# Requesting the experts' down weights on another engine's DMA queue in a hybrid block

## The chip, the cores and the metric

The kernel runs on one core of a Trainium2 chip. The metric is the device time of one execution in microseconds (us). The kernel before took 1451.0 us, the median of three runs (1449.7 to 1451.66).

A core has five engines that run their own instruction streams and meet at semaphores: PE (TensorE, matmuls; its weight loads are shown as PEld), DVE (VectorE), ACT (ScalarE), POOL (GpSimd) and SP (SyncE, which here only issues transfers). A transfer (DMA) is issued by SP, ACT or POOL and carried out by the core's 16 DMA engines.

## The reference, cut to what matters

One block on 1024 tokens of width 1024: a mixer (a gated delta rule beside a causal convolution), a mixture of experts, a gate, and a norm. The change lies in the mixture of experts:

```python
group_p = softmax(xf @ w_group_router); g_w, g_idx = top_k(group_p, 1)
in_group = (xf @ w_expert_router) of the chosen group of 8 experts
e_w, e_idx = top_k(softmax(in_group), 2)          # 2 of 64 experts for each token
gate = g_w * e_w / sum(e_w)
...
def expert_block(args):                            # x_blk: tokens of one expert
    x_blk, e = args
    a, b = jnp.split(x_blk @ w_up[e], 2, axis=-1)  # 1024 -> 2 x 256
    return (jax.nn.silu(a) * b) @ w_down[e]        # 256 -> 1024
...
y = segment_sum(yb * buf_w[:, None], buf_tok, num_segments=N)
```

All is float32. Per expert w_up is 1024 x 512 (2 MB) and w_down 256 x 1024 (1 MB), so the 64 experts bring 192 MB from HBM, once each.

## The kernel before

The program has stages one behind the other: norm and input projection, the delta rule, output projection and router logits, the routing tables, then the expert stage (`c7`, from line 1832), then the gate and final norm (`c8`, from line 2203).

In the expert stage the 64 experts are taken as 32 pairs; pair p holds the experts p and p + 32. Each expert has 64 token slots, so that one half of the 128 columns belongs to each. Work of one pair on PE, in this order: U(p), 16 up matmuls (line 2121) of 128x512 (the profile counts each as two); T(p+1), 8 transposes of the next pair's tokens (line 2110); 2 transposes of the hidden values (line 2130); D(p), 8 down matmuls (line 2142). ACT does, in order: `silu` of half of U(p) (line 1978), its half of the copy of T(p+1) (line 1974), and `result`, its half of the copy of D(p) out of PSUM (line 1984). DVE has the other halves. POOL gathers the tokens (line 1919) and scatters the results to `y_rows` (line 1925), by indirect transfers.

All weight buffers are double: `wup[k]` (in the `wup` ring) and `wdn[k]` (in `zT` for k = 0, in `convT` for k = 1) with k = p mod 2, each with two halves c = 0, 1, one for each expert of the pair. The pairs 0 and 1 are requested during the routing stage (lines 1622 to 1626). From then on SP waits for the end of U(p) and requests the two up halves of pair p+2 (`fetch_up`), waits for the end of D(p) and requests the two down halves of pair p+2 (`fetch_down`), and so on for p = 0 to 29 (`fetch_pairs`, line 1874). U(p) waits for `s_up[k]`, D(p) for `s_dn[k]`.

An expert with more than 64 tokens has overflow blocks. They are worked off between pair 15 and pair 16 (`MID` = 8 loop turns of two pairs); in this run there is one. Its weights `wup_x` and `wdn_x` are loaded at the start of the stage.

Behind its last pair SP requests the ten weight rows of the gate stage (line 1900, 512 KB each). The first two can go at once; the others wait for buffers. ACT splits them into high parts (`weights_high`, line 1995) in a fixed order with its last pairs: silu(30), tokens(31), weights 0 and 1, result(30), weights 2 to 4, silu(31), result(31), weights 5 to 9 (lines 2015 to 2026).

Of the kernel before, what the change touches and what calls it, by code (L numbers as in the profile page):

```python
# [14 lines left out]
ds = bass.ds  # L15
# [30 lines left out]
def hybrid_block_kernel(nc, x, p, g_mix, w_in, w_conv_qkv, a_log, dt_bias, g_gdn_out, b_glu,  # L46
# [20 lines left out]
    NPR = NE // 2  # L67
# [11 lines left out]
    def sem(name):  # L79
        return top.enter_context(nc.semaphore(name))  # L80
# [3 lines left out]
    def wait_alone(eng, sem_, value):  # L84

        eng.wait_ge(sem_, value)
        eng.sem_inc(s_turn, 1)
# [7 lines left out]
    with top:  # L95
# [48 lines left out]
        with ExitStack() as c1:  # L144
# [13 lines left out]
            @blk.sync  # L158
            def _(sp):
                for t in range(NT):  # L160
                    sp.dma_start(xs[:, t, :], x[0, t * P:(t + 1) * P, :]).then_inc(s_x[t], 16)
                    if t == 1:
                        sp.dma_start(gmix[:], g_mix[0].rearrange("(p j) -> p j", j=NJ)).then_inc(s_loaded, 16)
                        sp.dma_start(wraw[0][:], w_in_p[:, :, GOFF:GOFF + P]).then_inc(s_w[0], 16)
                sp.dma_start(wraw[1][:], w_in_p[:, :, GOFF + CF:GOFF + CF + P]).then_inc(s_w[1], 16)
# [525 lines left out]
        G2 = range(2)  # L691
# [876 lines left out]
        NS = 2  # L1568
        NJF = FE // P
        s_up = [sem(f"s_up{k}") for k in range(NS)]  # L1570
        s_dn = [sem(f"s_dn{k}") for k in range(NS)]
        wring = ExitStack()
        wup = [[sb(f"wup{k}{c}", [P, NJ, 2 * FE], ctx=wring) for c in G2] for k in range(NS)]
        wdn = [[t[:, c * NJF:(c + 1) * NJF, :] for c in G2] for t in (zT, convT)]
        up_p = w_up[0].rearrange("e (p j) n -> p e j n", j=NJ)
        dn_p = w_down[0].rearrange("e (p j) n -> p e j n", j=NJF)

        def fetch_up(sp, k, c, e):
            sp.dma_start(wup[k][c][:], up_p[:, e, :, :]).then_inc(s_up[k], 16)

        def fetch_down(sp, k, c, e):
            sp.dma_start(wdn[k][c], dn_p[:, e, :, :]).then_inc(s_dn[k], 16)
        s_iota, s_rv, s_ra, s_rp = sem("s_iota"), sem("s_rv"), sem("s_ra"), sem("s_rp")
        W8 = [P, NT, NG]
        with ExitStack() as c6:
# [215 lines left out]
        def wrow(j):  # L1801

            j -= p.shape[3] // P
            return w_ple_gate[0, j * P:(j + 1) * P, :] if j >= 0 else w_ple_proj[0, p.shape[3] + j * P:p.shape[3] + (j + 1) * P, :]
# [6 lines left out]
        s_T, s_x0, s_x1, s_u, s_sil, s_h, s_hT, s_hx, s_d, s_y0, s_y1 = (  # L1811
            sem("moe_" + n) for n in ("T", "x0", "x1", "u", "sil", "h", "hT", "hx", "d", "y0", "y1"))
# [16 lines left out]
        def fetch_rows(sp, t, g):  # L1829
            for y, k, there in ((yy[g], 0, s_fy[g]), (yz[g], 1, s_fz[g])):  # L1830
                sp.dma_start(y.unsqueeze(1), y_tok[ds(t * P, P), k:k + 1, :]).then_inc(there, 16)
        with ExitStack() as c7:
# [33 lines left out]
            @blk.sync  # L1866
            def _(sp):
                def fetch_over(v):
                    e = sp.value_load(eov[0:1, ds(v, 1)], min_val=0, max_val=NE - 1)
                    wait_alone(sp, s_od, v + 1)  # L1870
                    sp.dma_start(wup_x[:], up_p[:, ds(e, 1), :, :]).then_inc(s_oup, 16)
                    sp.dma_start(wdn_x[:], dn_p[:, ds(e, 1), :, :]).then_inc(s_odn, 16)

                def fetch_pairs(first_, last_):
                    with sp.Fori(first_, last_) as i:
                        for k in range(NS):
                            p = NS * i + k
                            wait_alone(sp, s_u, p + 1)
                            for c in G2:
                                fetch_up(sp, k, c, ds(p + NS + NPR * c, 1))  # L1880
                            wait_alone(sp, s_d, p + 1)
                            for c in G2:
                                fetch_down(sp, k, c, ds(p + NS + NPR * c, 1))

                n_over = sp.value_load(nov[0:1, 0:1], min_val=0, max_val=NOV)
                sp.sem_inc(s_od, 1)
                with sp.If(n_over > 0):
                    fetch_over(0)
                fetch_pairs(0, MID)
                with sp.If(n_over > 1):  # L1890
                    with sp.Fori(1, n_over) as v:
                        fetch_over(v)
                fetch_pairs(MID, NIT - 1)

                for j in range(NWJ):
                    if j >= NRAW:
                        sp.wait_ge(s_wg_lo, j - NRAW + 1)
                    elif j >= NAHEAD:
                        sp.wait_ge(s_T, NPR - NRAW + j + 1)
                    sp.dma_start(wg_raw[j % NRAW], wrow(j)).then_inc(s_wg[j % NRAW], 16)  # L1900
                    if j == NAHEAD:
                        for g in G2:
                            sp.dma_start(pin[g][:], p_tok[0, 0, g * P:(g + 1) * P, :]).then_inc(s_fp[g], 16)
                    if j == NRAW:
                        sp.wait_ge(s_d, NPR - 1)
                        sp.dma_start(gP, g_ple.partition_broadcast(P)).then_inc(s_gfin, 16)
                        sp.dma_start(gF, g_final.unsqueeze(0).partition_broadcast(P)).then_inc(s_gfin, 16)
                for k in range(NS):
                    sp.wait_ge(s_sto[k], 16 * NIT)
                sp.wait_ge(s_d, NPR)  # L1910
                for g in G2:
                    fetch_rows(sp, g, g)
# [57 lines left out]
            @blk.scalar  # L1970
            def _(act):
                def tokens(k, p):
                    act.wait_ge(s_T, p + 1)
                    nc.scalar.activation(xgT[k][:, 0:HJ, :], ps_x[0][:], ACT.Copy).then_inc(s_x0, 1)

                def silu(k, p, rows=slice(0, P)):
                    act.wait_ge(s_u, p + 1)
                    nc.scalar.activation(sil[k][rows], ps_u[k][rows, 0:FE], ACT.Silu).then_inc(s_sil, 1)  # L1978

                def result(k, p, free, rows=slice(0, P)):  # L1980
                    act.wait_ge(s_d, p + 1)
                    if free is not None:
                        act.wait_ge(s_sto[k], free)
                    nc.scalar.activation(ye[k][rows, HF[0]], ps_y[rows, 0, :], ACT.Copy).then_inc(s_y0, 1)

                def pair(i, k, last=False):
                    p = NS * i + k
                    silu(k, p)
                    if not last:
                        tokens(1 - k, p + 1)  # L1990
                    result(k, p, None if isinstance(i, int) and i == 0 else 16 * i)

                def weights_high(j):
                    act.wait_ge(s_wg[j % NRAW], 16 * (j // NRAW + 1))
                    nc.scalar.activation(wg[0][j], wg_raw[j % NRAW], ACT.Copy).then_inc(s_wg_hi, 1)

                tokens(0, 0)
                for k in range(NS):
                    pair(0, k)
                with act.Fori(1, MID) as i:  # L2000
                    for k in range(NS):
                        pair(i, k)
                n_over = act.value_load(nov[0:1, 0:1], min_val=0, max_val=NOV)
                with act.If(n_over > 0):
                    with act.Fori(0, n_over) as v:
                        act.wait_ge(s_oT, v + 1)
                        nc.scalar.activation(xgT_x[:, 0:HJ, :], ps_x[0][:, :, 0:C], ACT.Copy).then_inc(s_ox0, 1)
                        act.wait_ge(s_ou, v + 1)
                        nc.scalar.activation(sil_x[:], ps_u[0][HC[0], 0:FE], ACT.Silu).then_inc(s_osil, 1)
                        act.wait_ge(s_od, v + 2)  # L2010
                        nc.scalar.activation(ye_x[:, HF[0]], ps_y[HC[0], 0, :], ACT.Copy).then_inc(s_oy0, 1)
                with act.Fori(MID, NIT - 1) as i:
                    for k in range(NS):
                        pair(i, k)
                i, p = NIT - 1, NPR - NS
                silu(0, p)
                tokens(1, p + 1)
                for j in range(0, 2):
                    weights_high(j)
                result(0, p, 16 * i)  # L2020
                for j in range(2, N_X + 2):
                    weights_high(j)
                silu(1, p + 1)
                result(1, p + 1, 16 * i)
                for j in range(N_X + 2, NWJ):
                    weights_high(j)
# [397 lines left out]
```

## Time and profile before

| | us |
|---|---|
| median of three runs | 1451.0 |
| span of the profiled execution, first to last instruction | 1440.7 |
| expert stage, first U to last D | 752.0 to 1281.8 of the span |
| PE busy in the whole span | 1168.7 (81%) |
| weights of the up product, transfers | 64 of 2048 KB, and 1 for the overflow |
| weights of the down product, transfers | 64 of 1024 KB, and 1 for the overflow |
| moved in all by DMA | 272.67 MB |

The page does not give the profiled execution's own time beside its span; what lies around the span is 1451.0 - 1440.7 = 10.3 us if that execution took the median time. Read the page's slices first: each is 36 us long, and those of the expert stage (21 to 35) show whether PE or the DMA engines are full. Then the windows say the same in GB/s, the waits say for whom PE stood still, and the timeline gives the order of events inside one pair. A line "SPq ... DMA_DIRECT2D x2" is the issue of two transfers, not their duration: the transfer goes on long after it.

### The profile page before, as it was taken

To read this page: it belongs to the slowest core of one execution; us is meant where nothing else is said; L and a number is where in the kernel's file an instruction comes from. 1 tells how busy PE (TensorE), PEld (TensorE's weight loads), DVE (VectorE), ACT (ScalarE), POOL (GpSimd) and SP (SyncE) were. 2 spreads that over 40 slices of the span, in tenths; PEclk is the share of its full clock that TensorE was granted. 3 is DMA by queue.
4 is the path that set the end of the run, shared out by engine and by line. 5 is a ranking of instruction groups with operands and counts; after the bars stand their busy time and mean duration, and the time that the engine had idled before them with its cause. 6 is when DMAs were issued, how large, how long until landed. Compare 5 with 4: busy or idle time off the path is not lost. (4 is left out here: it accounts for less than half of the span.)

```text
span 1440.7 us, 17450 instructions
## 1 busy us (share of the span) xinstructions
PE 1168.7 (81%) x6323; PEld 774.1 (54%) x6324; DVE 635.6 (44%) x899; ACT 324.8 (23%) x691; POOL 242.4 (17%) x340
## 2 busy tenths in 40 slices
PE   4999999998578776999229888778888878748997
PEld 3888888895377665788213333223233333316775
DVE  7398989983476564522651111111111111144553
ACT  5221221214445443321101100101011100033222
POOL 2100000003445642000011111111112111111111
PEclk7999999976689899999559999989999999978999
DMA  4212111100000010411658999999799999962321
GB/s 148 60 44 58 44 44 44 44 0 0 1 1 2 4 57 17 154 70 61 267 207 336 427 428 425 421 406 413 305 419 428 426 425 417 417 227 75 108 95 44
DMA packets 68059, 272.67 MB, mean 189 GB/s; under 512 B 11625, under 2 KB 38442, under 8 KB 51370
## 3 DMA queue, kind: packets, MB, share of 16 engines
q1 hardware_dynamic: 56096, 254.30, 44.3%
q0 software_dynamic: 9456, 16.80, 3.1%
q10 hardware_dynamic: 2458, 0.92, 0.3%
q8 instruction: 30, 0.49, 0.1%
q14 instruction: 19, 0.16, 0.0%
HBM read 264.12 MB, written 25.43 MB: 201 GB/s over the span
## 5 line engine op out<-in xcount | busy, mean ns | idle before, releaser
L2121 PE MATMUL ps_u<-wup,xgT 128*64 128x512 f32 x1024 | 256.2, 658 | 60.6 <-DMA wup<-in_w_up_dram 58.0
L2121 PEld LDWEIGHTS ps_u<-wup,xgT 128*64 128x64 f32 x1024 | 85.7, 150 | 230.0 <-issue 228.8
L92 PE MATMUL ps_b<-n_hi,wh 128*128 128x512 f32 x384 | 150.5, 392 | 6.1 <-DVEq L405 6.1
L92 PE MATMUL ps_b<-n_lo,wh 128*128 128x512 f32 x384 | 150.2, 391 | 0.0
L92 PE MATMUL ps_b<-n_hi,wl 128*128 128x512 f32 x384 | 150.1, 391 | 0.0
L2041 DVE TENSOR_TENSOR hb<-sil,ps_u 128x256 f32<-128x256 f32 x32 | 13.5, 421 | 298.6 <-ACT sil L1978 298.6
L92 PEld LDWEIGHTS ps_b<-n_hi,wh 128*128 128x128 f32 x384 | 72.6, 189 | 21.4 <-ACTq L40 6.5
L92 PEld LDWEIGHTS ps_b<-n_hi,wl 128*128 128x128 f32 x384 | 72.6, 189 | 15.3
L92 PEld LDWEIGHTS ps_b<-n_lo,wh 128*128 128x128 f32 x384 | 72.7, 189 | 15.1
L1978 ACT ACTIVATE sil<-ps_u 128x256 f32<-128x256 f32 x32 | 12.2, 383 | 286.3 <-PE ps_u L2121 286.3
L423 DVE SCALAR_TENSOR_TENSOR convT<-upad,vecT,convT 128x1024 f32 (+1 forms) x60 | 76.7, 1278 | 0.0
L2053 DVE COPY qkvT<-ps_y 128x512 f32<-128x512 f32 x32 | 22.1, 690 | 122.1 <-PE ps_y L2142 122.1
L2142 PE MATMUL ps_y<-convT,hT 128*64 128x512 f32 x256 | 62.8, 635 | 12.2 <-DVE hT L2047 12.2
L423 DVE SCALAR_TENSOR_TENSOR odd<-upad,vecT,odd 128x1024 f32<-128x1024 f32 x56 | 71.5, 1277 | 0.0
L1923 POOL COPY si<-sidx 128x1 int32 (+1 forms) x32 | 6.6, 207 | 379.9 <-DVE qkvT L2053 379.9
L2142 PE MATMUL ps_y<-zT,hT 128*64 128x512 f32 x256 | 58.5, 598 | 11.0 <-DVE hT L2047 11.0
L357 ACT ACTIVATE wh<-wraw 128x1024 fp32r<-128x1024 f32 x24 | 25.5, 1062 | 172.4 <-PE ps_b L92 172.4
L92 PE MATMUL ps_o<-wo_hi,mix_hi 128*128 128x512 f32 x128 | 52.3, 408 | 6.6 <-DVE wo_lo L1485 6.4
L2110 PEld LDWEIGHTS ps_xg<-ident,xg 128*128 128x128 f32 x256 | 31.6, 195 | 46.2 <-issue 24.3
L601 POOL TENSOR_TENSOR GT<-sm_g,tri 128x512 f32<-128x512 f32 x8 | 8.0, 1038 | 287.3 <-DVE sm_g L657 287.3
L2110 PE MATMUL ps_xg<-ident,xg 128*128 128x128 f32 x256 | 37.9, 292 | 20.8 <-DMA xg<-xn_rows,gi 20.8
L92 PE MATMUL ps_gate<-wg_hi,hx_hi 128*128 128x512 f32 x128 | 51.7, 404 | 2.4 <-DVE hx_lo L2319 2.4
(368 smaller groups left out, 2034.6 us busy)
## 6 DMA issues: line engine op xcount, KB each, us to landing
wup<-in_w_up_dram SPq DMA_DIRECT2D x64, 2048.0 KB, 17.7
zT<-in_w_down_dram SPq DMA_DIRECT2D x32, 1024.0 KB, 17.3
convT<-in_w_down_dram SPq DMA_DIRECT2D x32, 1024.0 KB
wraw<-in_w_in_dram SPq DMA_DIRECT2D x25, 512.0 KB, 4.0
convT<-y_rows SPq DMA_DIRECT2D x16, 512.0 KB, 5.2
qkvT<-in_x_dram SPq DMA_DIRECT2D x8, 512.0 KB, 7.2
qkvT<-in_w_out_dram SPq DMA_DIRECT2D x8, 512.0 KB, 4.9
xr<-in_x_dram SPq DMA_DIRECT2D x8, 512.0 KB, 3.2
```

Of the source, the lines that this page charges most:

```text
L92: ins = nc.tensor.matmul(ps, lhs[a], rhs[b], start=first and k == 0, stop=last and k == 2)
L357: nc.scalar.activation(wh[n % 2][:], wraw[n % 2][:], ACT.Copy).then_inc(*a_proj(f"hi{n}"))
L423: ins = nc.vector.scalar_tensor_tensor(dst, src, DW(k, i), dst, ALU.mult, ALU.add)
L601: nc.gpsimd.tensor_tensor(GT[:, of_tile(t), :], sm["g"][:, t, :].unsqueeze(2).to_broadcast(F4), tri[:].unsqueeze(1).to_broadcast(F4), ALU. ...
L1923: nc.gpsimd.tensor_copy(si[k][:], sidx[:, p]).then_inc(s_idx, 1)
L1978: nc.scalar.activation(sil[k][rows], ps_u[k][rows, 0:FE], ACT.Silu).then_inc(s_sil, 1)
L2041: nc.vector.tensor_tensor(hb[k][rows], sil[k][rows], ps_u[k][rows, FE:2 * FE], ALU.mult).then_inc(s_h, 1)
L2053: nc.vector.tensor_copy(ye[k][rows, HF[1]], ps_y[rows, 1, :]).then_inc(s_y1, 1)
L2110: last = nc.tensor.transpose(ps_x[j // HJ][:, j % HJ, :], xg[k][:, j:D:NJ], ident[:])
L2121: last = nc.tensor.matmul(ps_u[k][HC[c], :], xgT[k][:, j, HC[c]], wup[k][c][:, j, :], start=j == 0, stop=j == NJ - 1)
L2142: last = nc.tensor.matmul(ps_y[HC[c], h, :], hT[k][:, f, HC[c]], wdn[k][c][:, f, HF[h]], start=f == 0, stop=f == NJF - 1)
```

## The change

`fetch_down` is called by ACT instead of SP. ACT calls it right behind `result(k, p)` in `pair`, for the same pairs (p = 0 to 29). SP no longer waits for the end of D(p). The transfers, their sizes, sources, targets and semaphores are the same.

```diff
-        def fetch_down(sp, k, c, e):
-            sp.dma_start(wdn[k][c], dn_p[:, e, :, :]).then_inc(s_dn[k], 16)
+        def fetch_down(eng, k, c, e):
+            eng.dma_start(wdn[k][c], dn_p[:, e, :, :]).then_inc(s_dn[k], 16)
...
                             wait_alone(sp, s_u, p + 1)
                             for c in G2:
                                 fetch_up(sp, k, c, ds(p + NS + NPR * c, 1))
-                            wait_alone(sp, s_d, p + 1)
-                            for c in G2:
-                                fetch_down(sp, k, c, ds(p + NS + NPR * c, 1))
...
                     result(k, p, None if isinstance(i, int) and i == 0 else 16 * i)
+                    for c in G2:
+                        fetch_down(act, k, c, ds(p + NS + NPR * c, 1))
```

On SP, in the body of the loop over pairs (two pairs a turn), before:

```order
L1579 DMA wup<-in_w_up_dram 128x4096
L1582 ISA
L1582 DMA zT<-in_w_down_dram 128x2048
L1582 ISA
L1582 DMA zT<-in_w_down_dram 128x2048
L1579 ISA
L1579 DMA wup<-in_w_up_dram 128x4096
L1579 ISA
L1579 DMA wup<-in_w_up_dram 128x4096
L1582 ISA
L1582 DMA convT<-in_w_down_dram 128x2048
```

The same place on SP after:

```order
L1579 DMA wup<-in_w_up_dram 128x4096
L1579 ISA
L1579 DMA wup<-in_w_up_dram 128x4096
L1579 ISA
L1579 DMA wup<-in_w_up_dram 128x4096
L1579 ISA
L1579 DMA wup<-in_w_up_dram 128x4096
L1875 REGISTER_ALU
L1875 COMPARE_AND_BRANCH
```

SP's queue now holds up weights alone, one pair's behind the other's. On ACT, in the body of its loop over pairs, before (`sil` is the silu, `xgT` the copy of the tokens, `qkvT<-ps_y` the result):

```order
L1978 ACTIVATE sil<-ps_u 128x256
L1973 REGISTER_ALU
L1974 ACTIVATE xgT<-ps_xg 128x512
L1983 REGISTER_ALU
L1984 ACTIVATE qkvT<-ps_y 128x512
L1978 ACTIVATE sil<-ps_u 128x256
```

and after:

```order
L1975 ACTIVATE sil<-ps_u 128x256
L1970 REGISTER_ALU
L1971 ACTIVATE xgT<-ps_xg 128x512
L1980 REGISTER_ALU
L1981 ACTIVATE qkvT<-ps_y 128x512
L1582 ISA
L1582 DMA zT<-in_w_down_dram 128x2048
L1582 ISA
L1582 DMA zT<-in_w_down_dram 128x2048
L1975 ACTIVATE sil<-ps_u 128x256
```

Two issues stand between the result of one pair and the silu of the next. The instructions of PE, DVE and POOL stand as before.

## Rows read from the trace of the kernel before

**Rows 1.** The page's 40 slices of 36 us: busy tenths, PE clock, DMA share and rate.

```profile
PE   4999999998578776999229888778888878748997
PEclk7999999976689899999559999989999999978999
DMA  4212111100000010411658999999799999962321
GB/s 148 60 44 58 44 44 44 44 0 0 1 1 2 4 57 17 154 70 61 267 207 336 427 428 425 421 406 413 305 419 428 426 425 417 417 227 75 108 95 44
```

**Rows 2.** Windows of the expert stage: length, busy by engine, clock, DMA share, GB/s.

```profile
762.00:810.00 48.00, 41.00 (x200) 16.28 (x198) 8.53 (x16) 6.07 (x12) 8.72 (x15) 0.99 0.99 408
810.00:1005.00 195.00, 157.87 (x684) 60.17 (x686) 24.91 (x47) 18.33 (x35) 27.86 (x45) 0.92 1.01 420
1022.00:1031.30 9.30, 7.72 (x36) 2.62 (x36) 0.68 (x1) 0.81 (x2) 1.34 (x3) 1.00 0.20 81
1032.00:1094.00 62.00, 55.16 (x252) 20.45 (x250) 10.25 (x20) 7.50 (x14) 11.05 (x19) 0.94 1.00 413
1094.00:1261.00 167.00, 135.09 (x580) 51.86 (x580) 20.65 (x39) 15.18 (x29) 23.19 (x38) 0.92 1.01 422
```

**Rows 3.** Waits of PE, 762 to 1270 us: total, times, longest.

```profile
PE ps_u L2121 <- DMA wup<-in_w_up_dram: 58.0, 22, 4.2
PE ps_y L2142 <- DVE hT L2047: 22.6, 31, 0.9
```

**Rows 4.** Timeline of pairs 14 and 15, start and duration, [idle before <- releaser].

```profile
978.42 8.78 PE L2121 MATMUL ps_u<-wup,xgT 128*64 128x512 f32 x32 [2.90 <-DMA wup<-in_w_up_dram]
...
987.46 0.86 SPq L1579 DMA_DIRECT2D wup<-in_w_up_dram  x2
...
989.41 3.65 PE L2142 MATMUL ps_y<-zT,hT 128*64 128x512 f32 x16 [0.68 <-DVE hT L2047]
993.20 0.60 ACT L1984 ACTIVATE qkvT<-ps_y 128x512 f32<-128x512 f32 x1 [4.26 <-PE ps_y L2142]
...
993.31 0.85 SPq L1582 DMA_DIRECT2D zT<-in_w_down_dram  x2
...
994.99 1.51 PE L2121 MATMUL ps_u<-wup,xgT 128*64 128x512 f32 x6 [1.92 <-DMA wup<-in_w_up_dram]
```

**Rows 5.** DMA, 1100 to 1240 us: share by queue, then KB each and landing.

```profile
q1 hardware_dynamic: 4948, 54.09, 91.5%
q0 software_dynamic: 2547, 5.06, 9.3%
...
wup<-in_w_up_dram SPq DMA_DIRECT2D x18, 2048.0 KB, 19.8
...
zT<-in_w_down_dram SPq DMA_DIRECT2D x8, 1024.0 KB, 21.3
...
xg<-xn_rows,gi POOLq DMA_INDIRECT x8, 14.0
```

**Rows 6.** Timeline of a pair at full speed, pair 2 into pair 3.

```profile
780.36 0.60 ACT L1984 ACTIVATE qkvT<-ps_y 128x512 f32<-128x512 f32 x1 [4.18 <-PE ps_y L2142]
...
787.23 0.38 ACT L1978 ACTIVATE sil<-ps_u 128x256 f32<-128x256 f32 x1 [6.27 <-PE ps_u L2121]
```

**Rows 7.** Timeline around the overflow block and behind it.

```profile
1023.95 7.09 PE L2121 MATMUL ps_u<-wup,xgT 128*64 128x512 f32 x32 [1.58 <-DVE qkvT L2083]
...
1031.28 0.86 SPq L1579 DMA_DIRECT2D wup<-in_w_up_dram  x2
...
1033.16 1.05 POOL L1919 DMA_INDIRECT xg<-xn_rows,gi  x1 [0.91 <-POOL gi L1917]
...
1046.07 1.16 PE L2110 MATMUL ps_xg<-ident,xg 128*128 128x128 f32 x8 [2.31 <-DMA xg<-xn_rows,gi]
...
1062.09 0.87 SPq L1579 DMA_DIRECT2D wup<-in_w_up_dram  x2
```

**Rows 8.** Timeline of the end of the stage.

```profile
1261.28 7.09 PE L2121 MATMUL ps_u<-wup,xgT 128*64 128x512 f32 x32 [1.35 <-DMA wup<-in_w_up_dram]
1267.19 1.06 ACT L1995 ACTIVATE wg_hi<-qkvT 128x1024 fp32r<-128x1024 f32 x1 [11.40 <-DMA qkvT<-in_w_ple_proj_dram]
...
1272.91 1.06 ACT L1995 ACTIVATE wg_hi<-qkvT 128x1024 fp32r<-128x1024 f32 x1 [0.19 <-DMA qkvT<-in_w_ple_gate_dram]
...
1273.87 0.36 ACT L1978 ACTIVATE sil<-ps_u 128x256 f32<-128x256 f32 x1
...
1276.82 5.01 PE L2142 MATMUL ps_y<-convT,hT 128*64 128x512 f32 x16 [0.52 <-DVE hT L2047]
```

## Prediction

> **What bounds the kernel now.** I read the page's slices first. From slice 22 to slice 34 the DMA row stands at 9 with one dent, and the rate at 406 to 428 GB/s, while PE has room [rows 1]. The windows say it closer: 420 GB/s at a share of 1.01 from 810 to 1005 us, and 422 GB/s at 1.01 from 1094 to 1261 us [rows 2]. The dent is the overflow block: 81 GB/s from 1022 to 1031.3 us. So the expert stage is two stretches in which the DMA engines are full, with some 9 us between them in which they are nearly idle because everything requested has landed and the next request comes only at the end of U(16), at 1031.28 us [rows 7].
>
> Next the waits of PE: 58.0 us in 22 waits for up weights, and none for down weights; before D it waits only for DVE's copy [rows 3]. Then the order of one pair [rows 4]: U(14) starts when its up weights land (978.42), the up request of pair 16 goes out at 987.46, D(14) runs from 989.41, its down request goes out at 993.31, U(15) starts on landing at 994.99, some 16.6 us behind U(14).
>
> Last, the order of transfers. All weights stand in one queue, SP's, in the order up(p), down(p), up(p+1), down(p+1). U(p) can start when up(p) is down; down(p) moves behind it, while U(p) runs. Both halves of a down transfer are 2 x 1024 KB = 2.10 MB, at 422 GB/s 5.0 us. U and the transposes take 10 to 11 us from the start of U to the start of D (978.42 to 989.41 [rows 4]), so down(p) lands before D(p) wants it. This order is the best one for a stage bound by transfers: what is wanted first moves first.
>
> **The change, part by part.**
>
> *Issue time.* SP loses a wait and two issues for each pair; it was not waited for. ACT gains two issues behind each result. On SP two such issues took 0.85 us [rows 4]; taken as the same on ACT, or even double, they fit between the result at 780.36 + 0.60 us and the silu at 787.23 us, for which ACT stood idle 6.27 us in a pair at full speed [rows 6]. Cost: 0. Were the cover gone, each pair would pay 0.85 us only in a stretch where PE sets the pace. The request itself goes out up to 1 us later than now, since it stands behind the copy; down weights have 5 us and more to spare.
>
> *Order of the transfers, the term that counts.* Down(p) is requested at the end of D(p-2), that is one period (16.6 us) and PE's wait before U(p) starts. Now it stands behind up(p) in the queue and cannot move. On a queue of its own it can. What happens to two queues with work is shown by POOL's gathers: they are issued when some 20 us of weights are queued, and land in 14.0 us, while a down transfer that is issued on SP's queue lands in 21.3 us [rows 5]. So the queues share the engines, and the later queue does not wait for the earlier one. And the rate stays at 422 GB/s with both in use [rows 2, 5], so sharing costs no bandwidth.
>
> Then down(p), 5.0 us of work, is served between parts of up(p-1) and up(p). Even at one part in three it needs about 3 x 5.0 = 15 us of the 16.6 + 1.9 us (PE's wait in rows 4) it has before U(p) starts. So all of it moves ahead of the last bytes of up(p), and U(p) starts 5.0 us later than it does now. In the middle of a full stretch that costs nothing further: each pair is later by the same 5.0 us, the period stays what the bytes make it. The price is paid once at the end of a stretch, where the bytes that used to move under the last U now move ahead of it.
>
> First stretch: U(15), D(15) and the overflow block come 5.0 us later, and so does the request at the end of U(16) that starts the engines again. They had nothing to do in the meantime: the dent grows from 9.3 to about 14 us. Cost: +5.0 us. Bounds: 0, if down(15) still lands last; +6.3 us, if part of down(16), requested 1.7 us before U(15) starts, moves ahead too, and the request reaches an engine without delay (1.7 us at half the engines is 0.9 us; I allow 1.3).
>
> The Trainium skill, "DMA: Bandwidth & Descriptors", section "Queues, rings and completion order", says that each DMA engine goes round between the queues it has work for, and drains a whole packet of one before it switches. The gathers' 14.0 us against 21.3 us agree with it. By it the sum would be the same 5.0 us, since an up half and a down half would alternate, and both down halves pass before the second up half.
>
> Second stretch: U(31) comes another 5.0 us later. But here the end is not set by U(31). ACT stands before weights 0, which land at 1267.19 us behind down(31), goes through weights 1 to 4 until 1272.91 + 1.06 us, and does silu(31) at 1273.87 us only then; U(31) had ended at 1261.28 + 7.09 = 1268.4 us [rows 8]. The landing of these rows is the end of all bytes, which a change of order does not move. Now: U(31) starts at 1261.28 + 5.0 + 5.0 = 1271.3, ends 1278.4; weights 4 are done at 1273.97 + 5.0 = 1279.0. So silu(31) follows at 1279.0, 0 us beyond the first stretch's shift. If the wait before U(31) is longer, the granted clock may be lower (it is 0.92 on the mean of the full stretches [rows 2]): U then takes 8.78 us, as U(14) did behind a wait of 2.90 us [rows 4], and silu(31) comes at 1280.1, +1.1 us. I take +0.3, bounds 0 and +1.1.
>
> *Gathers.* A third queue in use delays gathers by at most one down half at a time, 2.5 us. In a full stretch they have room. Behind the overflow block they have none: the gather issued at 1033.16 us makes PE wait 2.31 us, until 1046.07 [rows 7]. The engines then have, from 1032 us [rows 2], two pairs' weights, 12.6 MB or 30 us at 422 GB/s, and 33 us with the gathers and scatters between them (weights are 54.09 of 59.15 MB [rows 5]), until 1065 us. The next up request comes at 1062.09 us [rows 7], just in time, so a delay of PE there can go through in part. Down(18) is requested at about 1037 us and stands in SP's queue behind up(18) now; after, it may go before the gather. Bounds 0 and +2.5 us; I take +0.5, nearer to 0, since down halves are queued there today too and some 2 us are to spare.
>
> Sum: 5.0 + 0.3 + 0.5 + 0 = +5.8 us. The profiled span would go from 1440.7 to 1446.5 us. With the 10.3 us around it, the median goes from 1451.0 to 1456.8 us, +0.4%. Its own range, from the bounds of the four terms where the mechanism holds, is +4.5 to +10 us: 1455.5 to 1461.
>
> **The rivals.**
>
> *No change.* The order does not matter: the bytes are the same, the engines are full, and down(15) lands in time either way. For it speaks that the rate can't rise and that PE's waits are for bytes; against it the 9.3 us of nearly idle engines behind the first stretch, which turn any later end of U(15) into time. It needs a sharing in which down(p) gets next to nothing of the engines beside up transfers: to pass whole it needs 5.0 of 18.5 us, 27%, and any less costs in proportion. Time 1451. The Trainium skill, the same page, section "Issuing engines are not separate DMA queues", says that requests from several engines run on the same 16 DMA engines and save only the sequencer's time. Taken by itself that gives no change; it says nothing of what lands first.
>
> *Faster.* SP's queue is served first whenever it has work, so up(p) no longer stands behind down(p-1) either. Place: up(15) would land up to 5.0 us earlier, and U(15) with it; D(15) still has 5 us to spare for its own weights. The dent shrinks from 9.3 to 4.3 us, time 1451.0 - 5.0 = 1446. Against it: the gathers on a second queue are not served last (14.0 us against 21.3 us [rows 5]).
>
> *Slower by more: the engines run dry.* At the start of U(p) there are queued, instead of the rest of down(p), up(p+1) and down(p+1), only the last two: about 15 us. The next request comes at the end of U(p), 8.8 us later. That leaves some 5 us, where now it is 10. If the 16 engines are further apart than that, or gathers come late for each pair, each of the 22 pairs that wait today loses about 0.7 us: 15 us on top, 1472. For it: landings differ from pair to pair (waits up to 4.2 us [rows 3]); against it: 5 us is more than that.
>
> **How the numbers follow.** A difference under 0.2% (2.9 us) can't be told from none here. The forecast has 0.62, no change 0.18, faster 0.08, dry engines 0.12. The forecast's range lies above 0.2% almost wholly (I leave 0.03 of it below): slower 0.59 + 0.12 = 0.71, same 0.21 with it, faster 0.08. The range that holds 8 in 10 takes the forecast's, most of no change, and part of dry engines: 1450.5 to 1464.
>
> **What would show it.** In the changed trace: down transfers on ACT's queue that land in 10 to 16 us instead of 21.3; up landings about as before (19.8), since request and start of U shift together; the period of a full stretch within 0.3 us of now; rates of 420 and 422 GB/s; U(16) at about 1029 us instead of 1023.95; the idle dent 14 us long; U(31) at about 1271 us, with silu(31) at 1279. I am wrong on the mechanism if U(16) starts within 1.5 us of 1024, wrong on its one-time price if the period has grown, and wrong on the end if silu(31) waits for U(31) by several us.

## The result, and the profile after

| | kernel before | changed kernel |
|---|---|---|
| median of 20 runs each | 1449.68 us | 1455.14 us |
| ratio, 95% interval | | 1.0044 [1.0027, 1.0061] |
| span of the profiled execution | 1440.7 us | 1446.0 us |

The change costs 0.44%, 6.4 us of 1449.7. The forecast was +5.8 us. The place of the price holds, at the overflow block; what it is made of does not, so the nearness of the two numbers is in part luck, as the profile after and the experiments show. One of the 20 executions of the kernel before took 3338.41 us and is left out of the ratio.

In every execution of the runs the time lies 1.7 to 2.1 us above its span (1447.81 and 1446.0 us for the profiled one of the changed kernel), not 10.3 us. So the profiled execution of the kernel before took about 1442.5 us (an estimate), and both profiled executions are some 7 us faster than the median of their kernel. Each profile below is one execution.

The DMA rate of the full stretches is what it was, with a longer dent in the middle (the page's slices, to read against [rows 1]):

```profile
DMA  4212111100000011421648999999699999972321
GB/s 148 59 44 58 44 44 44 44 0 1 1 1 2 8 53 23 147 73 58 283 190 355 426 427 423 418 408 403 257 425 411 428 426 413 417 252 75 116 95 44
```

The waits of PE, 762 to 1275 us, against [rows 3]:

```profile
PE ps_xg L2109 <- DMA xg<-xn_rows,gi: 43.6, 22, 3.2
PE ps_u L2120 <- DMA wup<-in_w_up_dram: 25.6, 14, 2.9
```

This the prediction had not seen: PE now waits for tokens in 22 pairs, and less for up weights. The transfers of 1100 to 1240 us, against [rows 5], say why:

```profile
q1 hardware_dynamic: 2490, 36.31, 61.8%
q10 hardware_dynamic: 2436, 17.71, 30.3%
q0 software_dynamic: 2441, 4.57, 8.5%
...
wup<-in_w_up_dram SPq DMA_DIRECT2D x16, 2048.0 KB, 18.3
zT<-in_w_down_dram ACTq DMA_DIRECT2D x10, 1024.0 KB, 16.5
convT<-in_w_down_dram ACTq DMA_DIRECT2D x8, 1024.0 KB, 18.2
y_rows<-qkvT,si POOLq DMA_INDIRECT x9, 16.4
xg<-xn_rows,gi POOLq DMA_INDIRECT x9, 22.9
```

Down weights land in 16.5 to 18.2 us instead of 21.3. Gathers, which now share with two queues, land in 22.9 us instead of 14.0.

The overflow block, from pair 15 to pair 16 (timeline, against [rows 4, 7]):

```profile
999.00 7.09 PE L2120 MATMUL ps_u<-wup,xgT 128*64 128x512 f32 x32 [1.47 <-DMA wup<-in_w_up_dram]
...
1008.09 1.16 PE L2109 MATMUL ps_xg<-ident,xg 128*128 128x128 f32 x8 [1.99 <-DMA xg<-xn_rows,gi]
...
1014.20 0.85 ACTq L1582 DMA_DIRECT2D convT<-in_w_down_dram  x2
...
1016.21 0.38 ACT L2006 ACTIVATE xgT_x<-ps_xg 128x256 f32<-128x256 f32 x1 [1.56 <-issue]
1016.65 7.08 PE L2164 MATMUL ps_u<-wup_x,xgT_x 128*64 128x512 f32 x16 [1.61 <-ACT xgT_x L2006]
...
1030.77 7.09 PE L2120 MATMUL ps_u<-wup,xgT 128*64 128x512 f32 x32 [1.58 <-DVE qkvT L2082]
```

The last rows of the dent, in windows of 1 us (the last two numbers are the DMA share and GB/s). Kernel before:

```profile
1028.00:1029.00 1.00, 1.00 (x8) 0.31 (x5) 0.00 (x0) 0.00 (x0) 0.00 (x0) 1.00 0.12 49
...
1030.00:1031.00 1.00, 1.00 (x7) 0.18 (x3) 0.00 (x0) 0.00 (x0) 0.15 (x1) 1.00 0.12 49
1031.00:1032.00 1.00, 1.00 (x10) 0.94 (x8) 0.42 (x1) 0.38 (x1) 0.93 (x1) 1.00 0.06 25
1032.00:1033.00 1.00, 0.56 (x4) 0.32 (x2) 0.84 (x3) 0.60 (x1) 0.24 (x2) 1.00 1.26 229
```

Changed kernel:

```profile
1033.00:1034.00 1.00, 1.00 (x8) 0.41 (x6) 0.00 (x0) 0.00 (x0) 0.00 (x0) 1.00 0.10 41
1034.00:1035.00 1.00, 1.00 (x6) 0.30 (x4) 0.00 (x0) 0.00 (x0) 0.00 (x0) 1.00 0.02 8
...
1035.00:1038.00 3.00, 3.00 (x16) 0.96 (x12) 0.00 (x0) 0.10 (x1) 1.35 (x3) 1.00 0.01 0
1038.00:1039.00 1.00, 1.00 (x9) 0.88 (x9) 0.44 (x2) 0.30 (x2) 0.57 (x1) 1.00 0.01 0
1039.00:1040.00 1.00, 0.38 (x2) 0.19 (x2) 1.00 (x2) 0.58 (x1) 0.48 (x1) 1.00 1.23 246
...
1024.00:1039.00 15.00, 12.30 (x51) 4.70 (x52) 1.83 (x5) 1.14 (x4) 2.85 (x5) 1.00 0.14 58
```

A share of 0.12 of 16 engines is the work of two engines; the view gives the mean alone, so that it is the same two all along is inferred. In the kernel before such a rest is at work until about half a microsecond before the next request is served (0.12 up to 1031 us, 0.06 in the next window). In the changed kernel all 16 stand all but still from 1034 to 1039 us, 5 us (shares of 0.03 or less). The time in which most engines have nothing to do is 10 us long in the kernel before (1022 to 1032 us, mean share 0.19) and 15 us in the changed kernel (1024 to 1039 us). That is where the price lies.

The stage starts at another time in each execution (U(0) at 752.0 us before, 753.4 in the changed kernel), so the table below counts from the start of U(0), read from the timelines.

| us from U(0), profiled execution | U(15) | overflow U | U(16) | U(31) |
|---|---|---|---|---|
| kernel before | 243.0 | 257.9 | 272.0 | 509.3 |
| changed | 245.6 | 263.2 | 277.4 | 518.2 |
| early gathers on the changed kernel | 244.8 | 262.0 | 277.7 | 517.5 |
| early gathers on the kernel before | 242.4 | 257.3 | 271.4 | 509.0 |
| down on ACT, first half | 246.2 | 263.2 | 277.4 | 514.9 |
| down on ACT, second half | 242.6 | 257.5 | 271.6 | 513.2 |
| up transfers split, changed | 249.2 | 267.8 | 283.6 | 526.0 |
| all on ACT's queue | 244.2 | 261.4 | 277.3 | 519.5 |
| all on ACT's queue, gate weights too | 243.8 | 261.1 | 276.9 | 516.4 |
| pair 15 down first | 248.3 | 264.5 | 278.6 | 514.9 |
| pair 31 down first | 242.7 | 257.6 | 271.7 | 514.3 |

The experiments behind these rows follow. One pattern runs through them: each kernel of this table whose U(16) comes 4.9 to 11.7 us later costs 5.4 to 10.1 us, and none whose U(16) is in time costs anything clear of the scatter. The next table says what makes U(16) late, by the rows of each timeline: idle time before a matmul group, and the group's own duration. "Slower U" is a U that took 8.4 to 10.0 us where it took 7.1 in the kernel before.

| us later than in the kernel before | up to U(15) | U(15) to overflow U | overflow U to U(16) | sum |
|---|---|---|---|---|
| changed | 2.6 | 2.8: tokens 2.0, ACT 0.7 | 0.0 | 5.4 |
| down on ACT, first half | 3.2 | 2.2: tokens 1.4, ACT 0.7 | 0.0 | 5.4 |
| early gathers on the changed kernel | 1.8 | 2.3: slower U 1.6, ACT 0.7 | 1.6: slower U | 5.7 |
| up transfers split, changed | 6.2 | 3.7: slower U 3.0, ACT 0.7 | 1.8: slower U | 11.7 |
| all on ACT's queue, gate weights too | 0.8 | 2.4: slower U 1.7, ACT 0.7 | 1.7: slower U | 4.9 |
| pair 15 down first | 5.3 | 1.3: slower U | 0.0 | 6.6 |

The end of the stage, against [rows 8]:

```profile
1271.62 10.09 PE L2120 MATMUL ps_u<-wup,xgT 128*64 128x512 f32 x32 [2.88 <-DMA wup<-in_w_up_dram]
1274.02 1.06 ACT L1994 ACTIVATE wg_hi<-qkvT 128x1024 fp32r<-128x1024 f32 x1 [9.42 <-DMA qkvT<-in_w_ple_proj_dram]
...
1281.74 0.38 ACT L1975 ACTIVATE sil<-ps_u 128x256 f32<-128x256 f32 x1 [0.64 <-PE ps_u L2120]
...
1283.77 3.65 PE L2141 MATMUL ps_y<-convT,hT 128*64 128x512 f32 x16 [0.52 <-DVE hT L2046]
```

### The profile page after: what moved, and what is told of

It is laid out like the page before. It is cut to its first block and busy times, and to the rows that moved or that the text cites. A ratio compares the mean times of both kernels' runs of the same rounds, so it can differ in the third digit from the quotient of the medians.

```text
span 1446.0 us, 17414 instructions
## 1 busy us (share of the span) xinstructions
PE 1165.4 (81%) x6323; PEld 769.8 (53%) x6324; DVE 636.7 (44%) x899; ACT 325.1 (22%) x691; POOL 241.5 (17%) x340
## 5 line engine op out<-in xcount | busy, mean ns | idle before, releaser
L2120 PE MATMUL ps_u<-wup,xgT 128*64 128x512 f32 x1024 | 239.2, 622 | 28.0 <-DMA wup<-in_w_up_dram 25.6
L2120 PEld LDWEIGHTS ps_u<-wup,xgT 128*64 128x64 f32 x1024 | 77.7, 144 | 186.6 <-issue 185.4
L2109 PE MATMUL ps_xg<-ident,xg 128*128 128x128 f32 x256 | 40.9, 308 | 62.3 <-DMA xg<-xn_rows,gi 62.3
L2141 PE MATMUL ps_y<-zT,hT 128*64 128x512 f32 x256 | 76.3, 751 | 12.4 <-DVE hT L2046 12.4
## 6 DMA issues: line engine op xcount, KB each, us to landing
wup<-in_w_up_dram SPq DMA_DIRECT2D x64, 2048.0 KB, 16.8
zT<-in_w_down_dram ACTq DMA_DIRECT2D x30, 1024.0 KB, 16.5
```

The lines of the kernel that those rows point to most:

```text
L2109: last = nc.tensor.transpose(ps_x[j // HJ][:, j % HJ, :], xg[k][:, j:D:NJ], ident[:])
L2120: last = nc.tensor.matmul(ps_u[k][HC[c], :], xgT[k][:, j, HC[c]], wup[k][c][:, j, :], start=j == 0, stop=j == NJ - 1)
L2141: last = nc.tensor.matmul(ps_y[HC[c], h, :], hT[k][:, f, HC[c]], wdn[k][c][:, f, HF[h]], start=f == 0, stop=f == NJF - 1)
```

## The experiments

The expectations below name four theories. O: the price is that of the order of the transfers, down(p) moving ahead of up(p). G: it is that of the late gathers. P: each pair pays a part. I: issuing transfers on ACT costs by itself.

**In which stretch is it paid?** The loop turns ahead of the overflow block request down weights in one way, those behind it in the other:

```diff
-                def fetch_pairs(first_, last_):
+                def fetch_pairs(first_, last_, downs):
...
-                fetch_pairs(0, MID)
+                fetch_pairs(0, MID, False)
...
-                fetch_pairs(MID, NIT - 1)
+                fetch_pairs(MID, NIT - 1, True)
```

(with `fetch_down` called in ACT's `pair` for the turns where SP does not; the second kernel has the two the other way round).

> Down weights are requested on ACT's queue for pairs 2 to 17 only (the loop turns ahead of the overflow block), on SP's for 18 to 31. Theories O and G: the whole price is paid at the overflow block, where the DMA engines run empty, so +5 to +7 us as with the full change, and U(16) at about 1030 us. Rival P (a price for each pair): half of the full change, +2 to +3 us.

> Down weights are requested on ACT's queue for pairs 18 to 31 only, on SP's for 2 to 17. Theory O: U(31) starts 5 us later but ACT stands before the gate weights anyway, so 0 to +1.5 us, U(16) at 1024 us as before. Rival P (a price for each pair): +2 to +3 us.

Measured: first half 1.0057 [1.0026, 1.0088], second half 1.0000 [0.9975, 1.0026]. The price is paid in the first half, at the overflow block; in the second there is none to within some 4 us. A price of 2 to 3 us in each half falls, since the first half alone costs at least 3.8 us, and nothing shows that ACT's issues cost in the loop. In the second half U(31) came 3.9 us later (509.3 to 513.2) and PE waited 30.1 us for tokens, without an effect on the time that could be told from none.

**Are the late gathers the cause?** POOL's `turn` gathers pair p, then scatters pair p-3 instead of p-2:

```diff
-                    fetch_tokens(k, ds(p, 1), 2 * p - NS + 1)
-                    wait_alone(pool, s_y0, p - NS + 1)
-                    wait_alone(pool, s_y1, p - NS + 1)
-                    scatter(k, ds(p - NS, 1), 2 * p - NS + 2)
+                    gather(k, p)
+                    scattered(1 - k, p - NS - 1, 2 * p - NS + 1)
```

> The changed kernel with one thing more: POOL requests the tokens of pair p ahead of the scatter of pair p-3 and its wait for D(p-3), instead of behind them, so gathers go out 6 to 9 us earlier. Theory O (order of the weights): what costs is that down(p) moves ahead of up(p), +5 us once at the overflow block. Gathers in time only turn PE's waits for tokens (43.6 us in the changed kernel) back into waits for up weights; U(16) still starts at 1028 to 1029 us and the time stays 4 to 6 us above the kernel before. Theory G (late gathers): what costs is that tokens come late, so D(p) and the next down request come late; with tokens in time the kernel goes back to within 1 us of the kernel before.

> The kernel before with the earlier gathers alone. Both theories: PE's one wait for tokens behind the overflow block (2.31 us) is the only one that can go, and up weights set the pace elsewhere: 0 to 2 us faster than the kernel before. A change beyond 3 us would mean that gathers set something that the waits of before do not show.

Measured: on the changed kernel 1.0046 [1.0020, 1.0072], on the kernel before 0.9994 [0.9976, 1.0011]. The waits of PE in the changed kernel with early gathers, 750 to 1300 us, have none for tokens:

```profile
PE ps_u L2136 <- DMA wup<-in_w_up_dram: 64.6, 26, 3.8
PE ps_y L2157 <- DVE hT L2062: 23.0, 32, 0.8
```

So 43.6 us of waits for tokens can be taken away and the time stays: the forecast of theory G, within 1 us of the kernel before, fails. But the experiment changed more than PE's waits for tokens. In its profile gathers still take longer than in the kernel before (18.1 us for 14.0), down weights land almost as late as there, and the scatters take 20.9 us:

```profile
convT<-in_w_down_dram ACTq DMA_DIRECT2D x8, 1024.0 KB, 19.8
y_rows<-qkvT,si POOLq DMA_INDIRECT x9, 20.9
xg<-xn_rows,gi POOLq DMA_INDIRECT x8, 18.1
```

U(15) is only 1.8 us late, the 2.0 us for tokens are gone, and in their place stand two slower U's at the block (3.2 us). So the order of the weights does not carry the 5.7 us of this kernel by itself either, and what share of the changed kernel's price the gathers have is not settled by it.

**Order alone, on one queue.** SP requests pair 15, that one pair, in the other order (called with p = 13; the up halves then go out behind the end of D(13) too, about 6 us later than in the kernel before, while the engines stay full: a share of 1.01 from 980 to 1000 us):

```diff
+                def down_first(p):
+                    k = p % NS
+                    sp.wait_ge(s_u, p + 1)
+                    sp.wait_ge(s_d, p + 1)
+                    for c in G2:
+                        fetch_down(sp, k, c, p + NS + NPR * c)
+                    for c in G2:
+                        fetch_up(sp, k, c, p + NS + NPR * c)
```

> The kernel before, all requests on SP's queue, with one difference: for pair 15, the last ahead of the overflow block, SP waits for the end of U(13) and of D(13) and requests the down halves ahead of the up halves. Nothing is issued on ACT, gathers share with one queue. Theory O: this alone makes U(15) land 5.0 us later and brings the whole price of the first stretch: U(16) 4 to 6 us later against the stage's start, all 16 DMA engines idle for some 4 us before the next request, time +3 to +6 us. Theory G and rival I (gathers, or issuing on ACT): no change, 0 to +1 us.

> The same swap for pair 31, the last of the stage, alone. Theory O: U(31) starts 4 to 6 us later but ACT's silu(31) stands behind gate weights 2 to 4 anyway: 0 to +2 us. A rival in which any late U counts in full: +5 us.

Measured: pair 15 1.0037 [1.0018, 1.0057], pair 31 0.9979 [0.9956, 1.0001]. U(15) with pair 15 swapped:

```profile
1000.89 8.41 PE L2142 MATMUL ps_u<-wup,xgT 128*64 128x512 f32 x32 [9.66 <-DMA wup<-in_w_up_dram]
```

It starts 5.3 us later against U(0) (248.3 and 243.0), the 5.0 us of the sum, and U(16) 6.6 us later, the rest being a slower U(15) (8.41 for 7.09 us). As theory O expected, all engines stand all but still before the next request, from 1033 to 1038 us (a share of 0.02). One pair's order, with no second queue and nothing on ACT, costs 0.37% (0.18 to 0.57), about what the whole change does. At pair 31 the same shift (514.3 and 509.3, 5.0 us) costs nothing, since ACT reaches silu(31) late in any case. This shows that the order alone can bring such a price, and that a late U counts at the block and not at the end of the stage. It does not show that the order brings the whole of it in the changed kernel, where U(15) is 2.6 us late and not 5.3.

**The share that down weights get.** Each up transfer in two, of 8 KB pieces instead of 16 KB:

```diff
-            sp.dma_start(wup[k][c][:], up_p[:, e, :, :]).then_inc(s_up[k], 16)
+            for j in (0, NJ // 2):
+                sp.dma_start(wup[k][c][:, j:j + NJ // 2, :], up_p[:, e, j:j + NJ // 2, :]).then_inc(s_up[k], 16)
```

> The changed kernel with each up transfer of 2048 KB issued as two of 1024 KB (four of eight rows of a partition each, so the pieces are 8 KB long instead of 16 KB). Theory O+: queues take turns piece by piece, so down weights get an even share instead of a third and pass even earlier; the order price stays at +5 us, while gathers wait for shorter pieces and come back from 22.9 towards 14 to 17 us. Theory G: with gathers back in time the price goes, 0 to +2 us. If turns go by whole transfers the same holds; if they go by time or bytes, gathers stay at 23 us.

Measured: 1.0070 [1.0044, 1.0097]. Landings, 1100 to 1240 us:

```profile
convT<-in_w_down_dram ACTq DMA_DIRECT2D x8, 1024.0 KB, 12.2
y_rows<-qkvT,si POOLq DMA_INDIRECT x8, 10.3
xg<-xn_rows,gi POOLq DMA_INDIRECT x8, 13.2
```

Gathers are back at 13.2 us and down weights land in 12.2 instead of 18.2: with pieces of 8 KB on both queues down weights get the larger share. U(15) starts 6.2 us late (249.2) instead of 2.6. Gathers in time and yet a price: again against the forecast of G, for O. Whether the price is higher than the changed kernel's is not clear of the intervals, and of the 11.7 us by which U(16) is late 4.7 us are slower U's. The landings fit queues that take turns by piece; whole transfers as turns were not told apart from it by this run. Nor do the pieces alone set them: with early gathers the pieces are 16 and 8 KB as in the changed kernel, and gathers landed in 18.1 us there, not in 22.9.

**One queue again, on ACT.** ACT requests up weights too, behind its copy of the tokens; in the second kernel also the gate weights 0 to 2 and the first tiles of p:

```diff
+                    for c in G2:
+                        fetch_up(act, k, c, ds(p + NS + NPR * c, 1))
                     result(k, p, None if isinstance(i, int) and i == 0 else 16 * i)
                     for c in G2:
                         fetch_down(act, k, c, ds(p + NS + NPR * c, 1))
```

> All weights of the loop on one queue again, but ACT's: ACT requests the up halves of pair p+2 behind its copy of the tokens, the down halves behind its result; SP only keeps the waits. Theories O and G (two queues are the cause): order and gathers as before, down landings about 21 us, gathers about 14 us, U(16) within 1.5 us of 1024, time 0 to +2 us (ACT is held for its issues at the overflow block, 0.7 us in the changed kernel). Rival I (issuing on ACT is the cause): as slow as the changed kernel or slower, +5 us and more, since ACT now issues three times the bytes and twice the transfers.

> All weights of the loop on ACT's queue, and the gate weights 0 to 2 and the first two tiles of p behind them on the same queue, so that nothing passes up(31) from another queue at the end. Theory O: what was left of the price in the run without this (U(31) waited 5.2 us, silu(31) 10.7 us late) goes; what remains is ACT's 0.7 us at the overflow block and the clock that PE happens to have there: 0 to +4 us, between the kernel before and the run without this. Rival I (issuing on ACT itself costs): stays at +8 us.

Measured: 1.0058 [1.0034, 1.0082] and 1.0044 [1.0021, 1.0067]. I had expected 0 to +2 and 0 to +4 us: missed. Landings are as in the kernel before (down 20.3 to 21.1 us, gathers 14.2 and 13.8), U(15) is 1.2 and 0.8 us late, and yet U(16) is 5.3 and 4.9 us late. The timeline of the second kernel:

```profile
995.61 8.78 PE L2126 MATMUL ps_u<-wup,xgT 128*64 128x512 f32 x32 [2.09 <-DMA wup<-in_w_up_dram]
...
1012.44 0.38 ACT L2007 ACTIVATE xgT_x<-ps_xg 128x256 f32<-128x256 f32 x1 [1.54 <-issue]
1012.88 8.78 PE L2170 MATMUL ps_u<-wup_x,xgT_x 128*64 128x512 f32 x16 [1.60 <-ACT xgT_x L2007]
```

Three things are added: 0.8 us at U(15), 0.7 us because ACT issues its two down requests before it copies the overflow block's tokens (idle before U of the block 1.60 us, before 0.90), and 1.7 us twice, since both U(15) and the block's U took 8.78 us where they took 7.09 and 7.05 in the kernel before. 0.8 + 0.7 + 1.7 + 1.7 = 4.9 us. Behind U(16) there is one more: its up request goes out 8.4 us behind its start, not 7.3 as in the kernel before (1031.28 - 1023.95), since ACT issues it behind its copy. So issuing on ACT costs in this place (0.7 and 1.0 us shown), and the clock that PE has there 3.4 us. The granted clock (the third number from the end) during U(15) in the kernel before:

```profile
994.99:1002.10 7.11, 7.11 (x33) 2.71 (x34) 0.00 (x0) 0.00 (x0) 2.26 (x3) 1.00 0.99 407
```

and in the second kernel of this pair during U(15) and the block's U:

```profile
995.61:1004.40 8.79, 8.79 (x33) 3.19 (x33) 0.00 (x0) 0.00 (x0) 2.26 (x3) 0.81 0.99 409
1012.88:1021.66 8.78, 8.77 (x16) 2.48 (x16) 0.00 (x0) 0.00 (x0) 0.67 (x2) 0.81 1.00 397
```

1.00 is the upper of its two levels (2.4 GHz) throughout, 0.81 is a mean, with a part of the time at the lower one (1.2 GHz, shown as 0.50). Why PE is at the lower level there in both of these kernels and with early gathers (0.81 as well), and not in the kernel before, is open: its waits before U alternate between about 2 and 4 us in the kernel before and are 2 to 3 us in the two kernels here, and each kernel has one profile.

Rival I had forecast the size of both results (+5 us and more, +8 us; measured 8.4 and 6.4 us), so these two runs do not speak against it. What does is the second half (ACT issues there, 1.0000) and pair 15 (nothing on ACT, 1.0037): issuing on ACT is not the whole cause.

**The overflow block elsewhere.** `MID = 2`, so that it comes between pairs 3 and 4:

```diff
-            MID = NIT // 2
+            MID = 2
```

> The kernel before with the overflow block worked off between pairs 3 and 4 (MID = 2) instead of between 15 and 16. There the engines are not yet waited for (PE's first wait for up weights is at 810 us). The engines' idle dent of 9.3 us should be shorter, since up(4), down(4), up(5), down(5) are mostly still queued when the block begins: by all theories 3 to 9 us faster than the kernel before.

> The changed kernel with the overflow block between pairs 3 and 4. Theory O: the stretch ahead of the block is not bound by transfers, so nothing is paid there; at the end ACT's wait for gate weights covers the shift. The difference to the kernel before with the same move falls from +6.4 us to 0 to +2 us. Rival P (a price for each pair) and theory G in the form that late gathers cost each pair: the difference stays at +5 to +7 us.

Measured: 1.0025 [1.0004, 1.0046] and 1.0069 [1.0040, 1.0097]. Both misses, and of one kind. I took the dent of 9.3 us as idle time to be had. But the last two engines have almost none of it; that this is why nothing was gained is argued, and no run isolates it. With the block moved, such late work is still going on when the next request goes out at 836.13 us:

```profile
835.00:836.00 1.00, 1.00 (x7) 0.19 (x3) 0.00 (x0) 0.07 (x1) 0.18 (x1) 1.00 0.16 66
836.00:837.00 1.00, 1.00 (x9) 0.88 (x8) 0.42 (x1) 0.31 (x1) 0.45 (x1) 1.00 0.08 33
```

while in the changed kernel all engines stand all but still there too, for some 5 us:

```profile
825.00:830.00 5.00, 5.00 (x26) 1.61 (x22) 0.00 (x0) 0.00 (x0) 2.16 (x4) 1.00 0.02 2
```

The changed kernel's PE waits as early as U(3) (1.57 us for up weights) and T(4) (2.08 us for tokens), so the stretch ahead of the block is bound by transfers there, against my expectation, and its price is paid: U(4), the first behind the block, is 6.0 us late (75.8 us from U(0) for 69.8), and the two kernels' runs are 4.8 us apart on the mean (1454.5 and 1449.7 us), about what it is at the old place.

**A version that beats both.** The end of the stage in [rows 8] shows U(31) done at 1268.4 us and ACT elsewhere. On ACT, silu(31) goes ahead of gate weights 2 to 4, on DVE `hidden` and `hidden_turned` likewise:

```diff
+                silu(1, p + 1)
                 for j in range(2, N_X + 2):
                     weights_high(j)
-                silu(1, p + 1)
```

> The kernel before with silu(31) on ACT, and hidden(31) with its turned copy on DVE, ahead of the gate weights 2 to 4 instead of behind them. U(31) ends at 1268.4 us in the kernel before and silu(31) starts at 1273.87 us only because ACT is at those weights. Expected by every theory: D(31) ends 4 to 5.5 us earlier, the gate weights are done 0 to 2 us later, and the time falls by 2 to 5 us. If it stays, the gate stage waits for its last weight rows and not for D(31).

Measured: 0.9970 [0.9949, 0.9991] on the kernel before, 4.3 us less. In its profile silu(31) follows result(30) at once:

```profile
1273.78 0.38 ACT L1978 ACTIVATE sil<-ps_u 128x256 f32<-128x256 f32 x1
...
1276.85 5.76 PE L2142 MATMUL ps_y<-convT,hT 128*64 128x512 f32 x16 [0.52 <-DVE hT L2047]
```

D(31) starts 520.2 us behind U(0) (at 756.7) and 524.8 in the kernel before, 4.6 us earlier. The kernel with pair 31 swapped, of which no gain was expected, stands at 0.9979, so a part of the 4.3 us may be scatter.

## Why the prediction was right, point by point

*What bounds the kernel* held: DMA share about 1.0 in both full stretches after as before, and PE's waits only changed their name. One reading was wrong in it, "nearly idle because everything requested has landed": the mean share of 0.20 hid engines that fell silent one after the other, from a share of 0.39 at 1022 us to 0.12 at 1031, the work of two. The conclusion survived the error, since that rest ends just before the request: any later request leaves all 16 idle.

*Issue time, cost 0*, failed at one place. In the loop no cost shows (second half, 1.0000). At the overflow block nothing lies between ACT's issues and the copy that PE waits for: 0.7 us (idle before the block's U 1.61 us instead of 0.90).

*Order of the transfers, +5.0 us at the first stretch.* The place is right: U(16) is 5.4 us late against U(0), and all engines stand still for 5 us where in the kernel before a rest of work went on. The swap of one pair's order gives the +5.3 us at U(15) and 1.0037 in time. But in the changed kernel the term is mis-sized: U(15) is only 2.6 us late, half of the forecast. Down weights on their own queue land in 16.5 to 18.2 us at the median, about the 16.6 + 1.9 us they had, so some may not pass (that last step is argued, not shown). With the larger share that split up transfers give them, it is 6.2 us. The rest of the 5.4 us is 2.0 us of PE's wait for the tokens of pair 16, ahead of the block, and 0.7 us of ACT, and the sum had both at 0. All three delay the same request; that the two make up for the missing 2.4 us is luck.

*Gathers, +0.5 us behind the block, "in a full stretch they have room"*: this step failed. I took one down half, 2.5 us, as the most that a third queue can add; a gather took 8.9 us longer (14.0 to 22.9). So a gather gives way more than once, and in the full stretch, where the sum had no cost for it, it brings the 2.0 us above. The 0.5 us stood for the gather behind the block: PE waited 1.07 us there for tokens it had waited 2.31 us for, and 3.04 us for those of the next pair, for which it had not waited. That each of its small pieces waits its turn would explain it and is not shown.

By the Trainium skill, "DMA: Bandwidth & Descriptors", section "Queues, rings and completion order", queues take turns by packet; the prediction took a half transfer for such a packet. The 8.9 us are more than one down half (2.5 us) and agree with turns shorter than that, or with several turns for a gather; how long a turn is, no run here shows.

*The end, +0.3 us.* U(31) is 8.9 us late and ran for 10.09 us (a granted clock of 0.70 on the mean, so more than half of the time at the lower level), so silu(31) did wait for it, 0.64 us, as the bound of this term allowed. D(31) then ran in 3.65 us instead of 5.01. D(31) ends 4.2 us later against U(0), less than the 5.4 us that U(16) had lost: about -1 us here in these two profiles. The ratio of the half that holds it, [0.9975, 1.0026], can't tell that from +0.3.

*Of the signs named*: down landings of 10 to 16 us were 16.5 to 18.2, a miss that goes with the mis-sized order term; up landings 18.3 for 19.8; rates 418 and 419 GB/s for 420 and 422; the period kept (16.8 us from U(4) to U(15) in both); the dent 15 us for 14; U(16) at 1030.8 for 1029; U(31) at 1271.6 for 1271; silu(31) at 1281.7 for 1279. The last three are in the span's time, and the stage began 1.4 us later than in the kernel before.

*The range.* Its lower end of +4.5 us does not follow from the bounds of the terms, since the order term's own lower bound is 0. And the slack of the rival of dry engines is 15 - 8.8 = 6.2 us, not 5. Neither changes the result.

## What to carry to other kernels

Where transfers bound a stage, put what is waited for first on one queue, and keep what can wait behind it: here a second queue gave no rate (418 and 419 GB/s for 420 and 422) and took the order away. The wrong order cost nothing that could be measured inside a full stretch; it was paid once, where the stretch ended and the next request came later, so look for those places (here the wrong order of one pair of 32 was enough for 0.37%). Add up everything that delays that one request, the clock of PE too. And read a low DMA share as engines, not as time: 0.12 of 16 is the work of two engines that may be setting the pace.

## What the runs showed that I had not expected

- The work of two of the 16 engines ends some 5 to 10 us behind that of the others at the end of the first stretch (share 0.64 at 1020 us, 0.25 at 1025, 0.12 to 0.14 from 1026 to 1031, 49 to 57 GB/s, in the kernel before). Moving a block into the seeming gap gained nothing (1.0025).
- A gather of 128 rows took 8.9 us longer beside two queues of weights than beside one, at an all but unchanged total rate (419 for 422 GB/s), and came back to 13.2 us when the pieces of the larger transfer were halved. In the kernel that issues gathers earlier, beside the same two queues, it took 18.1 us.
- The same U took 7.09 us or 8.4 to 10 us at the overflow block in kernels that differ only in their requests, and in four of them this is 3.2 to 4.7 us of the lateness of U(16).
- Forty-odd us of waits of PE appeared or went (43.6 us for tokens in the changed kernel, none with early gathers) with no change of the time beyond the intervals.
